# Gate products of the recurrent branch: four 64-wide blocks on the quadrants of the array in place of two 128-wide products

## The chip, the cores and the metric

The kernel runs on one core of one Trainium2 chip. The metric is the device time of one execution in microseconds. The kernel before has a median of 1052.98 us over 3 runs (1050.32 to 1054.1). TensorE is called PE in the profile, its weight loads PEld, VectorE DVE, ScalarE ACT, GpSimd POOL, and the queue of SyncE, which issues the transfers, SPq.

## The reference

One inference step of a one-layer hybrid decoder, for a prompt of 512 positions and 8 sampled sequences of 4 positions each (T = 544 columns in all). What matters here is the recurrent branch (an RG-LRU):

```python
xb = xf.reshape(B, T, RNN_BLOCKS, RNN_BLOCK_W)          # 16 blocks of 64
r = sigmoid(einsum('btnc,ncd->btnd', xb, w_a) + b_a)    # gate r: 64x64 product in each block
i = sigmoid(einsum('btnc,ncd->btnd', xb, w_x) + b_x)    # gate i: the same with other weights
log_a = LRU_C * r * log_sigmoid(lam)
a = exp(log_a)
u = sqrt(-expm1(2.0 * log_a)) * (i * xf)
h[t] = a[t] * h[t-1] + u[t]                             # scan over the positions
branch_a = (h * gelu(gr)) @ w_rnn_out
```

Around it stand one combined input projection, a sparse attention branch with an index, a merge, a feed-forward network (D_FF = 2816) and an embedding gate. Everything is float32.

## The kernel before, in words

**Tiles and units.** All large projections go through one stream of weight units. A unit is up to 8 chunks of 128x128 weights, loaded by SPq into a ring of 4 (`wraw`), rounded by ACT (`round_weights`, L613) to `whi`, and its rest computed by POOL (`lower_weights`, L1549) as `wlo`. ACT and POOL do this four units ahead of TensorE. TensorE (`run`, L1759) makes three products for each chunk (`whi` with the high and low part of the operand, `wlo` with the high part), each in two halves of 272 columns, into one of two pairs of PSUM banks (`psD`). A tile's pair of banks is free again when ACT or DVE has read it (`tile_read`). `run_around(n, work)` runs the first half of a unit, then `work`, then the second half.

**The recurrent branch.** D_RNN is 1024, so 8 chunks (c = 0 to 7) of 128 channels, each with two blocks of 64. Chunk c needs an `xr` tile (input of the branch) and a `gr` tile (its GeLU gate). TensorE's order for one chunk is: first half of the tile `xr` c+1, gate products `gate_sums(c, 0)`, second half of that tile, `gate_sums(c, 1)`, tile `gr` c. For c = 7, the first half of the tile `gr` 7 stands before its first gate product. Two other small jobs lie between: the turns `spt` and `spn` of the sampled attention after chunk 0's gates, and `new_values` with `past_values` before chunk 1 and again after chunk 2 (L1960, L1969).

**Gate products.** The weights `bd` hold, for each chunk and gate, a 128x128 matrix with two 64x64 blocks on its diagonal and zeros elsewhere. The operand `xc` has EO = 568 columns, taken as two halves of EH = 284 (k = 0, 1). Each half is a job of its own in the order `plan_aux`: its results go to one of two PSUM banks in turn (`psX[0]`, `psX[1]`, named by `bank(job)`). `start_job` waits until the job two before it was read, `end_job` tells the reader. Each float32 product shows in the trace as two records.

**ScalarE's order for a chunk.** `gates(c, 0)`: two Tanh instructions from PSUM into `rq` (L800, 128x284 each, scale and bias by partition), then the decay factor (Exp, L807) and a Tanh (L809); `final_states(c-1)` (L832 to L836); `gates(c, 1)`: two more of L800 into `ig`; the square root (L622); `y_upper` (L843); `conv_line(c+1)` (L773 to L781), which copies the `xr` tile out of PSUM and makes the first tap of the convolution; one rounding of weights (L613); `initial_states` (L826); the GeLU (L817); one more rounding. Three loads of function tables lie in each chunk.

**VectorE's order for a chunk.** `recurrence(c)`: L1281, L1286, L1287, then a wait for the square root, L1289, L1292, L1295, the convolution taps of chunk c+1 (L1152, three instructions), L1299, the scan L1305; `branch(c)`: L1313, L1314. After chunk 6 also `sample_own` (L1266). At the end stands `sample_out_lo` (L1271); TensorE's second attention product (L2023, in tile `ga` 0) needs the bank that it reads.

Of the kernel before, what the change touches and what calls it, by code (L numbers as in the profile page):

```python
# [11 lines left out]
ACT = mybir.ActivationFunctionType  # L12

P = 128
D = 1024
DC = D // P
# [8 lines left out]
HD = 64  # L25
# [25 lines left out]
EO = EXT - (CW - 1)  # L51
EH = EO // 2
# [115 lines left out]
def hybrid_decoder_step(nc, a, o):  # L168
# [13 lines left out]
    def place(name, shape, dt=F32, over=None, plus=0):  # L182

        size = 4 * int(np.prod(shape[1:]))
        if over is None:
            spot[name] = free[0]
            free[0] += (size + 31) // 32 * 32
        else:
            spot[name] = spot[over] + plus
        assert spot[name] + size <= 229344, (name, spot[name] + size - 229344)  # L190
        return nc.alloc_sbuf_tensor_at(name, shape, dt, offset=spot[name])
# [24 lines left out]
    lru = place("lru", [P, 8, DC])  # L216
    stat = place("stat", [P, 64])
    sstat = place("sstat", [P, 8])
    top8 = place("top8", [P, 8])
    pt = place("pt", [1, NB * NPG], I32)  # L220
    hmul = [place(f"hmul{i}", [P, T]) for i in range(2)]
# [37 lines left out]
    bd = place("bd", [P, DC, 2, P], F32, "iqT")  # L259
# [37 lines left out]
    with ctx:  # L297
# [62 lines left out]
        def bank(job):  # L360
            return psX[AUX[job] % 2]
# [23 lines left out]
        def got_job(eng, job):  # L385
            eng.wait_ge(aux_done, AUX[job] + 1)

        def read_job(ins, job):
            return ins.then_inc(aux_read[AUX[job] % 2], 1)
# [205 lines left out]
        def _(act):  # L595
            sc = nc.scalar
# [149 lines left out]
            def sample_exp(g):  # L746
                job_read(act, ("smask", g))
                sc.activation(ps_s[:, g, :], ps_s[:, g, :], ACT.Exp, bias=sstat[:, g:g + 1], scale=-1.0,
                              accum_out=sstat[:, 2 + g:3 + g]).then_inc(sexp_ok, 1)
# [34 lines left out]
            def gates(c, which):  # L784

                s = c % 2
                if which:
                    pass
                elif c >= 2:
                    act.wait_ge(hs_ok, c - 1)  # L790
                elif c == 0:
                    act.wait_ge(lru_v, 1)
                    job_read(act, ("vout", TT))
                else:
                    act.wait_ge(sp_ok, 2)
                for g, dst in (((0, rq[s]), (1, ig[s]))[which],):
                    for k in range(2):
                        job = ("gate", c, g, k)
                        got_job(act, job)
                        read_job(sc.activation(dst[:, EH * k:EH * (k + 1)], bank(job)[:, 0:EH], ACT.Tanh, scale=0.5,  # L800
                                               bias=lru[:, 4 + g, c:c + 1]), job)
                    if g == 0:
                        job_read(act, ("gate", c, 0, 0))
                        job_read(act, ("gate", c, 0, 1))
                        if c:
                            act.wait_ge(u_w, c)
                        sc.activation(dec[c // 5][:], rq[s][:], ACT.Exp, scale=lru[:, 6, c:c + 1],  # L807
                                      bias=lru[:, 6, c:c + 1]).then_inc(dec_ok, 1)
                        sc.activation(rq[s][:], rq[s][:], ACT.Tanh, scale=lru[:, 3, c:c + 1],  # L809
                                      bias=lru[:, 3, c:c + 1]).then_inc(q_lru, 1)  # L810
# [43 lines left out]

            sample_exp(0)
            sample_exp(1)
            for c in range(DC):
                gates(c, 0)
                if c >= 1:
                    final_states(c - 1)  # L860
                gates(c, 1)
                if c == 0:
                    sample_turned()
                lru_root(c)
                if c >= 1:
                    y_upper(c - 1)
                if c + 1 < DC:
                    conv_line(c + 1, NTH[("xr", c + 1, False)])
                    round_weights(n + RING)
                    n += 1  # L870
                initial_states(c)
                gelu_path(c, NTH[("gr", c, False)])
                round_weights(n + RING)
                n += 1
# [823 lines left out]
        def _(pe):  # L1698
            te = nc.tensor

            def start_job(job):

                n = AUX[job]
                if n >= 2:
                    pe.wait_ge(aux_read[n % 2], n // 2)
                return bank(job)

            def end_job(ins):
                return ins.then_inc(aux_done, 1)
# [236 lines left out]

            def gate_sums(c, g):

                for k in range(2):
                    b = start_job(("gate", c, g, k))  # L1950
                    if g == 0 and k == 0:
                        pe.wait_ge(xc_ok, c + 1)
                        if c == 0:
                            pe.wait_ge(bd_in, 64)
                    end_job(te.matmul(b[:, 0:EH], bd[:, c, g, :], xc[c % 2][:, EH * k:EH * (k + 1)],  # L1955
                                      start=True, stop=True))

            def new_values(g):

# [231 lines left out]
```

## Time and profile before

| | |
|---|---|
| median of 3 runs | 1052.98 us (1050.32 to 1054.1) |
| the profiled execution | 1053.02 us, of which the span of the core's instructions is 1051.3 us |
| mean granted clock of TensorE | 0.985 |
| stretch of the recurrent chunks | about 203 to 322.5 us of the span |
| gate products | 32 matmuls (64 records at L1955), 16 calls of `gate_sums` |

In the rows below, times are in us from the start of the span. A row of the timeline gives start, duration, engine, line, operation, output and inputs, shapes and the number of instructions that were merged into the row; in brackets stands how long the engine was idle before it and what ended that. In matmul rows, "128\*64" is the part of the array in use, rows by columns.

### The profile page before, as it was taken

The page shows a single profiled execution, that of the slowest core. Times are in us where ns is not written, and L with a number is a line of the kernel's source. Part 1 is how long each engine was busy: PE and PEld are TensorE (multiplying, and loading weights), DVE is VectorE, ACT ScalarE, POOL GpSimd, SP SyncE. Part 2 cuts the span into 40 slices and gives each one's busy share as a digit, 9 for nine tenths or more (in the row PEclk, how much of TensorE's full clock was granted, in tenths as well). Part 3 has the DMA queues.
Part 4 walks back from the last instruction along what each step waited for, and adds up shares of the span by engine and source line. Part 5 has one row for each costly group of instructions (what it writes and reads, how often), then busy time and mean ns, then how long its engine had stood idle before and what let it go on. Part 6 is the DMA issues. An engine that isn't in the chain of part 4 may idle for free.

```text
span 1051.3 us, 19192 instructions
## 1 busy us (share of the span) xinstructions
PE 1004.3 (96%) x7811; PEld 960.9 (91%) x7811; DVE 489.8 (47%) x762; ACT 421.0 (40%) x705; POOL 448.3 (43%) x301
## 2 busy tenths in 40 slices
PE   4889999899997999999999999999999999999997
PEld 3876898689996999899999999999999999999996
DVE  2315899478995344324454433343001333334464
ACT  5424333578994434333332522222112223233534
POOL 2513352156886445424541543433334433344530
PEclk9898999999998999999999999999999999999999
DMA  6633356542232431333252422322333232122502
GB/s 187 185 50 87 100 152 184 172 121 80 72 83 54 101 94 30 80 92 92 80 176 71 140 81 80 99 66 75 91 104 101 88 93 72 51 88 59 161 1 86
DMA packets 168751, 101.98 MB, mean 97 GB/s; under 512 B 12626, under 2 KB 160754, under 8 KB 168418
## 3 DMA queue, kind: packets, MB, share of 16 engines
q1 hardware_dynamic: 168674, 100.91, 34.2%
q8 instruction: 54, 0.88, 0.4%
q14 instruction: 23, 0.19, 0.1%
HBM read 93.26 MB, written 7.63 MB: 96 GB/s over the span
## 4 chain that ended last, share of the span: by engine, by line
PE 89%; ACT 3%; DVE 3%; DMA 3%; issue 1%; SPq 1%; POOL 1%; ACTq 0%; DVEq 0%
PE psD L1759 80%; PE psX L1713 2%; DMA wraw<-in_w_in 1%; PE held L1713 1%; PE psX L2023 1%; PE held L2047 1%; PE psX L1842 1%; PE psX L1955 1%; DMA prm<-in_state_rglru_h 1%; ACT whi L613 1%; DMA kpg<-in_cache_k 0%; PE held L1912 0%; PE held L1969 0%; POOL h_lo L1555 0%; DVE xc L1152 0%
## 5 line engine op out<-in xcount | busy, mean ns | idle before, releaser
L1549 POOL TENSOR_TENSOR wlo<-wraw,whi 128x1024 fp32r<-128x1024 f32 (+5 forms) x213 | 388.6, 1836 | 548.4 <-ACT whi L613 548.3
L1759 PE MATMUL psD<-h_hi,whi 128*128 128x272 f32 (+1 forms) x1616 | 344.9, 295 | 5.0 <-POOL h_lo L1555 3.1
L1759 PE MATMUL psD<-h_hi,wlo 128*128 128x272 f32 (+1 forms) x1616 | 336.4, 290 | 0.0
L1759 PE MATMUL psD<-h_lo,whi 128*128 128x272 f32 (+1 forms) x1616 | 335.8, 289 | 0.0
L1759 PEld LDWEIGHTS psD<-h_hi,whi 128*128 128x128 f32 (+1 forms) x1616 | 256.4, 190 | 17.4 <-issue 10.9
L1759 PEld LDWEIGHTS psD<-h_lo,whi 128*128 128x128 f32 (+1 forms) x1616 | 256.1, 190 | 0.0
L613 ACT CAST whi<-wraw 128x1024 fp32r<-128x1024 f32 (+4 forms) x165 | 154.8, 939 | 251.4 <-PE psD L1759 224.0
L1759 PEld LDWEIGHTS psD<-h_hi,wlo 128*128 128x128 f32 (+1 forms) x1616 | 254.5, 190 | 0.0
L1759 PE MATMUL psD<-act_hi,whi 128*128 128x272 f32 x672 | 140.8, 291 | 0.0
L1759 PE MATMUL psD<-act_hi,wlo 128*128 128x272 f32 x672 | 139.0, 288 | 0.0
L1759 PE MATMUL psD<-act_lo,whi 128*128 128x272 f32 x672 | 138.6, 288 | 0.0
L1759 PEld LDWEIGHTS psD<-act_hi,whi 128*128 128x128 f32 x672 | 105.6, 189 | 0.5 <-DVE act_lo L1384 0.3
L1759 PEld LDWEIGHTS psD<-act_lo,whi 128*128 128x128 f32 x672 | 105.6, 188 | 0.0
L1759 PEld LDWEIGHTS psD<-act_hi,wlo 128*128 128x128 f32 x672 | 105.0, 189 | 0.0
L1001 ACT ACTIVATE sg<-sg 128x544 f32<-128x544 f32 x22 | 14.5, 659 | 111.2 <-DVE sg L1450 111.2
L1499 DVE TENSOR_TENSOR x<-x,psD 128x544 f32<-128x544 f32 x16 | 11.5, 721 | 99.5 <-PE psD L1759 99.5
L1478 DVE TENSOR_TENSOR hmul<-sg,psD 128x544 f32<-128x544 f32 x22 | 15.9, 721 | 85.1 <-PE psD L1759 85.1
L1481 DVE TENSOR_TENSOR act_lo<-hmul,act_hi 128x544 f32 (+1 forms) x20 | 44.6, 2228 | 18.4 <-ACT act_hi L935 18.4
L1450 DVE TENSOR_TENSOR sg<-rb,psD 128x544 f32<-128x544 f32 x30 | 21.6, 721 | 67.4 <-PE psD L1759 67.4
L1335 DVE CUSTOM_DVE_ANT_0 pr<-psX,tm 128x128 f32<-128x128 f32 (+3 forms) x32 | 15.6, 489 | 63.7 <-PE held L1713 28.1
L892 ACT COPY pT<-held 128x128 f32<-128x128 f32 (+3 forms) x32 | 13.6, 424 | 46.4 <-PE held L1713 46.4
L916 ACT ACTIVATE sg<-psD 128x544 f32<-128x544 f32 x16 | 10.0, 625 | 50.0 <-PE psD L1759 50.0
(272 smaller groups left out, 975.2 us busy)
## 6 DMA issues: line engine op xcount, KB each, us to landing
wraw<-in_w_in SPq DMA_DIRECT2D x48, 512.0 KB, 4.6
wraw<-in_w_ffn_gate SPq DMA_DIRECT2D x22, 512.0 KB, 3.8
wraw<-in_w_ffn_up SPq DMA_DIRECT2D x22, 512.0 KB, 3.8
wraw<-in_w_ffn_down SPq DMA_DIRECT2D x16, 384.0 KB, 3.3
wraw<-in_w_ffn_down SPq DMA_DIRECT2D x16, 320.0 KB, 3.1
kpg<-in_cache_k SPq DMA_DIRECT2D x16, 256.0 KB, 3.0
wraw<-in_w_rnn_out SPq DMA_DIRECT2D x8, 512.0 KB, 5.0
wraw<-in_w_o SPq DMA_DIRECT2D x8, 512.0 KB, 5.9
```

The costliest lines, as they stand in the source:

```text
L613: sc.copy(whi[:, n % RING, 0:rc, 0:cc], wraw[:, n % RING, 0:rc, 0:cc]).then_inc(w_hi, 1)
L892: sc.copy(pT[s % 2][:, 0:block_of(s) + 1, :].rearrange("p k t -> p (k t)"), psX[2][:, 0:w])\
L1001: sc.activation(sg[k % 2][:], sg[k % 2][:], ACT.Silu).then_inc(act_ok, 1)
L1335: read_job(v.tensor_tensor_reduce(pr[st % 3][:, 0:w], bank(("qk", st))[:, 0:w], tm[st % 2][:, 0:w], -1.0, 3.0e38, ALU.add, ALU.min, stat[: ...
L1450: read_tile(v.tensor_tensor(two(sg[k % 2][:]), two(rb[:]), acc(t), ALU.mult), t)
L1478: read_tile(v.tensor_tensor(two(hmul[k % 2][:]), two(sg[k % 2][:]), acc(t), ALU.mult), t)
L1481: v.tensor_tensor(chunk(act_lo, f - 1), hmul[(k - 1) % 2][:], chunk(act_hi, f - 1).bitcast(F32), ALU.subtract).then_inc(f_lo, 1)
L1499: read_tile(v.tensor_tensor(two(x[:, j, :]), two(x[:, j, :]), acc(t), ALU.add), t)
L1549: ins = g_.tensor_tensor(wlo[:, s, r0:r1, 0:cc], wraw[:, s, r0:r1, 0:cc], whi[:, s, r0:r1, 0:cc].bitcast(F32), ALU.subtract)
L1713: return te.transpose(out, src, ident[0:rows, 0:rows])
L1759: ins = te.matmul(psD[0:cc, b0 + half, 0:HT], w[:, s, c, 0:cc], m[:, k0 + c, HT * half:HT * (half + 1)], start=(part == 0 and c == 0 and w ...
L1842: end_job(te.matmul(b[:, 0:P * (i + 1)], iqT[head_rows(h), h // 2, P * i:P * (i + 1)], ik2[head_rows(h), 0:P * (i + 1)], start=True, stop= ...
```

## The change

Each gate product of 128x128 (half of which are zeros) by 284 columns becomes two products of 64x64 blocks by the same 284 columns. For the first half of the columns (k = 0) block 0 stands on the upper left quadrant of the array and block 1 on the lower right, so that the results lie in PSUM as before. For the second half (k = 1) block 0 stands on the upper right quadrant and block 1 on the lower left: the results of block 0 come out on partitions 64 to 127 and those of block 1 on 0 to 63. The k = 1 results are read by two Tanh instructions of 64 partitions each, which take them crosswise, from partitions 64 to 127 into 0 to 63 of the destination and the other way round; the k = 0 results are read by one instruction as before. As the bias of such an instruction lies with its input, ScalarE makes a copy `crossed` of the two bias columns with the halves exchanged, in two small copies ahead of chunk 0. `gate_sums` now waits for both banks before its first product, not for each bank before its own.

```diff
+    crossed = place("crossed", [P, 2, DC])
...
                 for g, dst in (((0, rq[s]), (1, ig[s]))[which],):
-                    for k in range(2):
-                        job = ("gate", c, g, k)
-                        got_job(act, job)
-                        read_job(sc.activation(dst[:, EH * k:EH * (k + 1)], bank(job)[:, 0:EH], ACT.Tanh, scale=0.5,
-                                               bias=lru[:, 4 + g, c:c + 1]), job)
+                    job = ("gate", c, g, 0)
+                    got_job(act, job)
+                    read_job(sc.activation(dst[:, 0:EH], bank(job)[:, 0:EH], ACT.Tanh, scale=0.5,
+                                           bias=lru[:, 4 + g, c:c + 1]), job)
+                    job = ("gate", c, g, 1)
+                    got_job(act, job)
+                    for i, j in ((0, HD), (HD, 0)):
+                        ins = sc.activation(dst[i:i + HD, EH:EO], bank(job)[j:j + HD, 0:EH], ACT.Tanh, scale=0.5,
+                                            bias=crossed[j:j + HD, g, c:c + 1])
+                    read_job(ins, job)
...
             sample_exp(0)
             sample_exp(1)
+            act.wait_ge(lru_v, 1)
+            sc.copy(crossed[HD:P, :, :], lru[0:HD, 4:6, :])
+            link(sc.copy(crossed[0:HD, :, :], lru[HD:P, 4:6, :]))
...
             def gate_sums(c, g):
 
+                b = [start_job(("gate", c, g, k)) for k in range(2)]
+                if g == 0:
+                    pe.wait_ge(xc_ok, c + 1)
+                    if c == 0:
+                        pe.wait_ge(bd_in, 64)
                 for k in range(2):
-                    b = start_job(("gate", c, g, k))
-                    if g == 0 and k == 0:
-                        pe.wait_ge(xc_ok, c + 1)
-                        if c == 0:
-                            pe.wait_ge(bd_in, 64)
-                    end_job(te.matmul(b[:, 0:EH], bd[:, c, g, :], xc[c % 2][:, EH * k:EH * (k + 1)],
-                                      start=True, stop=True))
+                    for h in range(2):
+                        i, j = HD * h, HD * (h ^ k)
+                        ins = te.matmul(b[k][j:j + HD, 0:EH], bd[i:i + HD, c, g, i:i + HD],
+                                        xc[c % 2][i:i + HD, EH * k:EH * (k + 1)], start=True, stop=True,
+                                        tile_position=(i, j))
+                    end_job(ins)
```

## Rows read from the trace of the kernel before

**Rows 1.** The page: busy time of the engines, and the chain that ended last.

```profile
PE 1004.3 (96%) x7811; PEld 960.9 (91%) x7811; DVE 489.8 (47%) x762; ACT 421.0 (40%) x705; POOL 448.3 (43%) x301
PE psD L1759 80%; PE psX L1713 2%; DMA wraw<-in_w_in 1%; PE held L1713 1%; PE psX L2023 1%; PE held L2047 1%; PE psX L1842 1%; PE psX L1955 1%; DMA prm<-in_state_rglru_h 1%; ACT whi L613 1%; DMA kpg<-in_cache_k 0%; PE held L1912 0%; PE held
```

**Rows 2.** Windows: length; busy PE, PEld, DVE, ACT, POOL; PEclk; DMA share, GB/s.

```profile
278.40:292.40 14.00, 14.00 (x107) 13.60 (x106) 13.39 (x17) 12.98 (x24) 11.33 (x10) 1.00 0.28 76
306.40:322.50 16.10, 10.44 (x75) 9.35 (x73) 15.33 (x22) 11.38 (x24) 15.19 (x15) 0.91 0.38 98
```

**Rows 3.** Timeline of TensorE behind its last gate product.

```profile
322.53 0.79 PE L2023 MATMUL psX<-kT,qT 64*128 64x128 f32 x2 [5.31 <-DVE act_lo L1271]
```

**Rows 4.** Timeline of ScalarE, chunk 6 and the start of chunk 7.

```profile
293.06 0.92 ACT L800 ACTIVATE rq<-psX,lru 128x284 f32<-128x284 f32 x2 [0.74 <-PE psX L1955]
297.26 0.87 ACT L800 ACTIVATE ig<-psX,lru 128x284 f32<-128x284 f32 x2
299.44 0.68 ACT L622 ACTIVATE sq<-rq 128x568 f32<-128x568 f32 x1
307.01 0.92 ACT L800 ACTIVATE rq<-psX,lru 128x284 f32<-128x284 f32 x2 [0.72 <-PE psX L1955]
```

**Rows 5.** Timeline of VectorE, chunks 5 and 6.

```profile
295.00 1.68 DVE L1313 TENSOR_TENSOR hmul<-hs,hmul 128x512 f32<-128x512 f32 x1
300.23 0.78 DVE L1289 TENSOR_SCALAR rq<-dec 128x568 f32<-128x568 f32 x1
308.96 0.69 DVE L1313 TENSOR_TENSOR hmul<-hs,hmul 128x512 f32<-128x512 f32 x1
```

**Rows 6.** Timeline of TensorE around a call of the gate products.

```profile
220.28 0.42 PE L1759 MATMUL psD<-h_hi,wlo 128*128 128x272 f32 x2
220.53 1.12 PE L1955 MATMUL psX<-xc,bd 128*128 128x284 f32 x4
221.74 0.41 PE L1759 MATMUL psD<-h_lo,whi 128*128 128x272 f32 x2
```

**Rows 7.** Timeline of TensorE: column tiles of 32, and their last weight loads.

```profile
215.58 0.62 PE L1969 MATMUL held<-kpg,pts 128*32 128x512 f32 x2
215.59 0.62 PE L1969 MATMUL held<-vpg,pts 128*32 128x512 f32 x2
216.03 0.60 PE L1969 MATMUL held<-kpg,pts 128*32 128x512 f32 x2
...
215.62 0.12 PEld L1969 LDWEIGHTS held<-vpg,pts 128*32 128x32 f32 x2
```

**Rows 8.** Timeline of TensorE: row tiles of 64 (L1842), column tiles of 64 (L2047).

```profile
109.14 0.41 PE L1759 MATMUL psD<-h_hi,wlo 128*128 128x272 f32 x2
109.48 1.13 PE L1842 MATMUL psX<-ik,iqT 64*128 64x512 f32 x4
110.89 0.42 PE L1759 MATMUL psD<-h_lo,whi 128*128 128x272 f32 x2
...
460.40 1.09 PE L2047 MATMUL held<-pT,vtok 128*64 128x128 f32 x16 [1.70 <-ACT pT L892]
461.78 0.41 PE L1759 MATMUL psD<-act_lo,whi 128*128 128x272 f32 x2
```

**Rows 9.** ScalarE: one reading of 284 columns; 64 partitions read crosswise.

```profile
L800 ACT ACTIVATE ig<-psX,lru x16: 475/482/492, 206.3 to 311.6; 128x284 f32<-128x284 f32 x16
...
L681 ACT COPY ik<-psD 64x544 f32<-64x544 f32 x1 | 0.6, 605 | 0.0
```

**Rows 10.** Timeline of ScalarE: chunk 0, and the heads of chunks 1 and 3.

```profile
203.81 0.89 ACT L800 ACTIVATE rq<-psX,lru 128x284 f32<-128x284 f32 x2 [5.07 <-PE psX L1955]
206.31 0.86 ACT L800 ACTIVATE ig<-psX,lru 128x284 f32<-128x284 f32 x2
221.27 0.92 ACT L800 ACTIVATE rq<-psX,lru 128x284 f32<-128x284 f32 x2 [5.30 <-PE psX L1955]
251.22 0.92 ACT L800 ACTIVATE rq<-psX,lru 128x284 f32<-128x284 f32 x2 [1.99 <-PE psX L1955]
```

## The prediction

> **What bounds the kernel now.** I read the page first: TensorE is busy 96% of the span, the chain that ended last is 80% its large products, and the gate products are 1% of it [rows 1]. A saving on TensorE counts only where nothing else paces it. So next I cut the stretch of the recurrent chunks into windows. In chunk 5's 14.0 us TensorE is busy throughout, but VectorE is busy 13.39 us and ScalarE 12.98 us of the same stretch [rows 2]. Three engines run in step here, which the page's averages (47% and 40%) hide. Last the chain in order of time and the timeline of its end: from chunk 6's gate products the chain leaves TensorE and runs through ScalarE and VectorE to L1271, and TensorE, which had by then been idle for 5.31 us, goes on at 322.53 [rows 3]. What the branch costs is decided there, and by VectorE.
>
> How tight the three are: ScalarE waits 0.74 and 0.72 us for TensorE at the heads of chunks 6 and 7, which are 307.01 - 293.06 = 13.95 us apart [rows 4]; its own work in a loop is therefore 13.95 - 0.72 = 13.23 us. Its square root of chunk 6 ends at 299.44 + 0.68 = 300.12 [rows 4], and VectorE's L1289, which needs it, starts at 300.23 [rows 5]. From there to L1271 the timeline shows VectorE without a wait for anyone. What comes late to it in chunk 6 stays late.
>
> **TensorE's part.** Pairs of large products start 0.25 us apart. Without the gate call the second pair after the one at 220.28 would have started at 220.78; it starts at 221.74, so a call costs 0.96 us: four passes of 0.24 us and no change-over [rows 6]. After the change a call has 8 passes of 284 columns (4 products, two records each). Do they run side by side? Column tiles do: at L1969 the passes of four tiles start within 0.01 us of each other and the next ones 0.45 us later [rows 7], so 284 of those 512 columns take about 0.24 us, as above. Row tiles do as well: a call at L1842 has four passes of 512 columns, 4 x 0.43 = 1.72 us in turn, yet it moves the pairs behind it by only 110.89 - 109.64 = 1.25 us [rows 8]. The array split both ways is not in this trace. I take that it composes: 2 x 0.24 = 0.48 us of streaming.
>
> The change-over has a price. Of the 1.25 us at L1842, 0.86 is streaming; 0.39 is left [rows 8]. At L2047 16 passes of 128 columns stream two by two in 8 x 0.107 = 0.86 us; the second pair behind them starts 1.38 us after the first pass, where 0.86 + 0.25 would do, so the way out costs 0.27, and with the 0.09 us gap at L1842's way in (109.48 where 109.39 would do) it is 0.36 [rows 8]. A call then costs 0.48 + 0.36 to 0.39 = 0.84 to 0.87 us and saves about 0.1 us, not the half that the streaming suggests. I take 0.11, since two rows of the same kind agree. The bounds: no change-over at all gives 0.48 and saves 0.48; one unhidden load (0.12 us [rows 7]) on top of 0.87 gives 0.99 and loses 0.03.
>
> **ScalarE's part.** One reading of 284 columns lasts 0.482 us [rows 9] and two in a row 0.87 [rows 4], so one more in a row costs 0.39. Half the partitions do not look cheaper: a copy of 64x544, taken crosswise, lasted 0.605 us, while 284 columns on 128 partitions last 0.482 [rows 9], so the time goes by columns and a fixed part. I take the full 0.39; half of it would be the lower bound. Each gate call thus adds 0.39 us, 0.78 us a chunk. A bit comes back: the first pair of a chunk takes 0.92 us, since its second product comes late; arriving together they would take 0.87 [rows 4]. ScalarE's loop becomes 13.23 + 0.78 - 0.05 = 13.96 us, TensorE's 13.95 - 0.22 = 13.73. ScalarE takes over the pace, at about the old period. The two copies of `crossed` stand in 5.07 us for which ScalarE waits ahead of chunk 0 [rows 10] and cost nothing; without that cover they would be two short instructions, under 1 us (two readings), once.
>
> The rows above make the emptying of PSUM dearer by 0.39 us a call. The Trainium skill, TensorEngine Tiling (Array Packing), PSUM Bottleneck, speaks against the change in the same sense: tiling speeds up TensorE but not the emptying of PSUM, which may become the bottleneck. By that page alone the streaming would shrink and the pace would pass to ScalarE, which is what these rows give.
>
> **Chunk 0.** Here TensorE waits for ScalarE. The `ig` readings start at 206.31 behind three instructions [rows 10]; with three `rq` readings they start at 206.70. The turn `spt` needs the bank of the first of them (+ 0.39), `spn` that of the second: free at 206.31 + 0.39 + 0.48 = 207.18 now, at 206.70 + 0.78 + 0.48 = 207.96 then. TensorE leaves chunk 0 about 0.75 us late, and the saving of this chunk's two calls is lost in the waits.
>
> **Then chunk by chunk**, shifts against before. Chunk 1: ScalarE had 5.30 us of slack [rows 10], so TensorE decides: 0.75 - 0.11 = + 0.64. Chunk 2 (slack taken as the usual 0.73): ScalarE is ready at 0.64 - 0.73 + 0.73 = + 0.64, TensorE at 0.75 - 3 x 0.11 = + 0.42, so + 0.64. Chunk 3: ScalarE's slack was 1.99 [rows 10], so TensorE decides: 0.75 - 5 x 0.11 = + 0.20. Chunks 4 to 7 at ScalarE's pace, + 0.01 each: + 0.23 at chunk 6, + 0.24 at chunk 7. In chunk 6 both longer groups of readings stand ahead of the square root, which comes 0.23 + 0.78 = 1.0 us later; L1289 follows it, and the end of the branch comes 1.0 us later. Chunk 7's root, at 0.24 + 0.78, asks for the same.
>
> TensorE's own saving (13 calls from chunk 1 on, 1.4 us) only lengthens its idle stretch from 5.3 to about 5.3 + 1.4 - 0.75 + 1.0 = 7 us [rows 3]. The granted clock in this stretch is 0.91 of full already [rows 2], so the slow restart is in the time before too and I add nothing for it. Other waits that move, at no cost: GpSimd and the loads of weights stand behind ScalarE's roundings, about 1 us later but made four units of 6 us ahead; an `xr` tile's banks are read about 1 us later, and if TensorE stalls for them it eats only of its lead.
>
> **The sum.** The profiled execution took 1053.02 us, as good as the median: 1053.0 + 1.0 = 1054.0 us. Its own uncertainty: VectorE's instructions stretch when they fall on other work (L1313 took 1.68 us in chunk 5, 0.69 in chunk 6 [rows 5]), and a shift of 1 us deals these anew, by up to 2 us either way over the last two chunks. The three runs before spread over 3.8 us. About 0.5% (5.3 us) is what a measurement of this kernel can tell from no change.
>
> **Rivals.**
> 1. *Change-over nearly free*: 0.48 us a call. For it, only the bound; against it, both kinds of tiles pay 0.36 to 0.39 [rows 8]. TensorE is then at 0.75 - 0.48 = + 0.27 in chunk 1; ScalarE decides chunk 3 at 0.27 + 2 x 0.73 - 0.73 - 1.99 = - 0.99, chunk 6 at - 0.96, its root at - 0.96 + 0.78 = - 0.2: 1052.8 us. ScalarE gives all of it back. With readings at half the price or lucky overlaps on VectorE (- 2), down to 1050.8. Together 0.13.
> 2. *The halves take turns*, and it ends slower. The tiles of k = 0 and k = 1 share rows of the array; if each pair ran only after the other, a call would be 4 x 0.24 + 0.37 = 1.33 us, or 1.45 with an unhidden load: + 0.37 to + 0.49. It decides from about 1.1 us a call on, where TensorE's loop passes ScalarE's new one. Chunk 7 then starts at 0.75 + 13 x 0.37 to 0.49 = + 5.6 to + 7.1, its root 0.78 later: 1059.4 to 1060.9. Against it: the four tiles at L1969 share all rows and start together [rows 7]. Chance 0.10. The Trainium skill, TensorE: Matmul & The Clock Gate, What overlaps and what doesn't, says that weight loads overlap running products only when the row group differs; by that rule this rival comes true. The trace disagrees for column tiles: the last load of four tiles on the same rows starts at 215.62, within 0.04 us of their first pass [rows 7].
> 3. *No overlap on quadrants*: 8 x 0.24 + 0.37 = 2.29 us, + 1.33 a call, in all 0.75 + 13 x 1.33 + 0.78 = + 18.8: 1072 us. Only the lack of a row with the array split both ways speaks for it. 0.05.
>
> **How the numbers follow.** My forecast 0.66 (1052 to 1056.5), rival 1 0.13, rival 2 0.10, rival 3 0.05, something not named 0.06, half to each side. Faster by over 0.5% means below 1047.7 and has only the unnamed: 0.03. Slower by over 0.5% (above 1058.2) is rivals 2 and 3 and 0.02 of the unnamed: 0.17. Within: 0.80. The range 1050.5 to 1059.7 holds rival 1 and the near edge of rival 2 and leaves out some 0.17.
>
> **What would show it.** Right: a gate call moves the pairs of L1759 behind it by 0.8 to 0.9 us; the passes at L1955 start in two groups of four; three readings take about 1.26 us; ScalarE's idle time ahead of `rq` is gone in chunks 4 to 7; VectorE waits for the root in chunk 6; TensorE is idle for 6.5 to 7.5 us ahead of L2023, which goes on near 323.5. Wrong: passes in four groups or one by one, a ScalarE that still waits, L2023 before 321, or a longer stretch at a low clock after it.

## The result, and the profile of the changed kernel

The changed kernel takes 1061.01 us (median of 4 runs, 1059.94 to 1062.07), the kernel before, measured beside it, 1052.08 us (4 runs, 1050.32 to 1054.1): ratio 1.0078, 95% interval 1.0064 to 1.0092. It is slower by some 0.8%, clear of the noise, and the time lies above the predicted range. The profiled execution took 1060.13 us; its span is 1058.4 us where it was 1051.3.

The page of the changed kernel, busy time of the engines, against [rows 1]:

```profile
PE 1004.8 (95%) x7875; PEld 956.2 (90%) x7875; DVE 489.0 (46%) x762; ACT 431.3 (41%) x723; POOL 448.1 (42%) x301
```

ScalarE has 10.3 us more work in 18 more instructions, and TensorE's busy time has not fallen. The line hardly shows a loss of 7 us; the stages do.

TensorE of the changed kernel, timeline around a call of the gate products (as [rows 6]), then chunk 0, then a call late in the branch and the restart (as [rows 3]):

```profile
221.89 0.41 PE L1768 MATMUL psD<-h_hi,wlo 128*128 128x272 f32 x2
222.23 0.71 PE L1966 MATMUL psX<-xc,bd 64*64 64x284 f32 x8
...
223.23 0.42 PE L1768 MATMUL psD<-h_lo,whi 128*128 128x272 f32 x2
...
202.44 0.71 PE L1966 MATMUL psX<-xc,bd 64*64 64x284 f32 x8
204.93 0.71 PE L1966 MATMUL psX<-xc,bd 64*64 64x284 f32 x8 [1.78 <-ACT rq L805]
206.93 1.63 PE L1722 MATMUL psX<-ident,ps_s 128*128 128x128 f32 x6 [1.29 <-ACT ig L800]
208.22 0.80 PE L1768 MATMUL psD<-h_hi,whi 128*128 128x272 f32 x2
208.81 0.66 PE L1768 MATMUL psD<-h_lo,whi 128*128 128x272 f32 x2
209.27 0.66 PE L1768 MATMUL psD<-h_hi,wlo 128*128 128x272 f32 x2
...
295.92 0.71 PE L1966 MATMUL psX<-xc,bd 64*64 64x284 f32 x8 [0.68 <-DVE xc L1161]
...
327.78 0.79 PE L2036 MATMUL psX<-kT,qT 64*128 64x128 f32 x2 [4.25 <-DVE act_lo L1280]
```

Chunk 0 of the kernel before, for the waits and the distances:

```profile
203.04 1.12 PE L1955 MATMUL psX<-xc,bd 128*128 128x284 f32 x4
204.35 1.22 PE L1955 MATMUL psX<-xc,bd 128*128 128x284 f32 x4 [0.19 <-ACT rq L800]
206.84 0.87 PE L1713 MATMUL psX<-ident,ps_s 128*128 128x128 f32 x6 [1.26 <-ACT ig L800]
207.47 0.50 PE L1759 MATMUL psD<-h_hi,whi 128*128 128x272 f32 x2
```

Three things are to be seen. A call moves the second pair behind it to 223.23, where 221.89 + 0.50 would do without it: it costs 0.84 us, as forecast. In chunk 0 the longest wait is 1.78 us, where it was 1.26, and pairs of large products start 0.46 us apart in place of 0.25: TensorE came back from its waits at a lower clock. And late in the branch TensorE now waits 0.68 us for `xc`, the convolution's result on VectorE, and restarts at 327.78, where it had been 322.53.

ScalarE of the changed kernel, timeline of chunk 5 and the head of chunk 6, against [rows 4]:

```profile
282.27 0.50 ACT L800 ACTIVATE rq<-psX,lru 128x284 f32<-128x284 f32 x1
282.79 1.00 ACT L805 ACTIVATE rq<-psX,crossed 64x284 f32<-64x284 f32 x2
...
287.07 0.49 ACT L800 ACTIVATE ig<-psX,lru 128x284 f32<-128x284 f32 x1
287.58 1.00 ACT L805 ACTIVATE ig<-psX,crossed 64x284 f32<-64x284 f32 x2
...
296.72 0.50 ACT L800 ACTIVATE rq<-psX,lru 128x284 f32<-128x284 f32 x1
```

No row has a bracket: ScalarE waits for nobody, from head to head 14.45 us (before 13.95). The readings of a gate last 282.79 + 1.00 - 282.27 = 1.52 us; two lasted 0.87 to 0.92, and the forecast for three was 1.26. Each starts 0.50 to 0.52 us after the one ahead, which is its whole duration: the overlap that made "one more in a row" cost 0.39 is gone.

VectorE of the changed kernel, chunk 5, against [rows 5]:

```profile
290.68 0.46 DVE L1298 TENSOR_SCALAR rq<-dec 128x568 f32<-128x568 f32 x1 [0.65 <-ACT sq L623]
...
292.92 2.85 DVE L1161 SCALAR_TENSOR_TENSOR xc<-xe,prmT,xc 128x568 f32<-128x568 f32 x3 [0.34 <-ACT xc L782]
```

VectorE waits for the square root and for the first tap, both of ScalarE. TensorE waits for VectorE, ahead of the first gate call of chunks 2 and 4 to 7. Only at the heads of chunks 1 and 3 does ScalarE still wait for TensorE, 6.10 and 1.10 us. Everywhere else the branch runs at ScalarE's pace.

Windows of the changed kernel: chunk 0, the end of the branch (as the second of [rows 2]), the output turns at the end of the program:

```profile
202.40:210.40 8.00, 4.93 (x33) 3.54 (x33) 1.95 (x3) 6.76 (x12) 0.00 (x0) 0.79 0.57 165
...
311.20:327.70 16.50, 10.73 (x74) 9.74 (x74) 15.21 (x22) 12.51 (x26) 14.38 (x15) 0.85 0.35 97
...
1046.95:1058.40 11.45, 6.90 (x34) 6.25 (x34) 4.15 (x8) 4.33 (x7) 0.00 (x0) 0.65 0.51 196
```

The same windows of the kernel before, chunk 0 and output turns:

```profile
203.00:211.00 8.00, 6.55 (x44) 5.42 (x43) 2.43 (x6) 6.71 (x14) 0.00 (x0) 1.00 0.56 170
1041.10:1051.30 10.20, 5.52 (x34) 4.56 (x34) 3.87 (x8) 4.32 (x7) 0.00 (x0) 0.77 0.57 218
```

The granted clock was 1.00 in chunk 0 and is 0.79. In the output turns (the last transposes on TensorE, ahead of the outputs), which the diff doesn't touch, the same 34 matmuls take 6.90 us in place of 5.52, at 0.65 in place of 0.77 of the 2.4 GHz.

**Where the time came from.** Cutting both timelines at the first reading of chunks 0, 1 and 7, at the restart, at the next product of L2036 and at the sums ahead of the output turns gives the table. All kernels of the study stand in it (one profiled execution each, us):

| kernel | chunk 0 | chunks 1 to 7 | 7 to restart | restart to next | middle | output turns |
|---|---|---|---|---|---|---|
| before | 17.46 | 85.74 | 15.52 | 8.35 | 710.22 | 10.20 |
| changed | 19.76 | 88.16 | 16.59 | 8.94 | 710.23 | 11.45 |
| before, again | 17.47 | 85.74 | 15.51 | 8.49 | 710.25 | 10.25 |
| changed, again | 20.93 | 88.15 | 16.60 | 9.60 | 710.22 | 11.27 |
| e1 TensorE's part | 18.91 | 84.41 | 15.63 | 9.46 | 710.24 | 11.39 |
| e9 ScalarE's part | 19.78 | 88.72 | 16.59 | 8.86 | 710.24 | 11.46 |
| e2 straight halves | 19.69 | 88.53 | 16.29 | 9.07 | 710.23 | 11.46 |
| e15 upper half first | 18.63 | 88.43 | 16.58 | 8.82 | 710.22 | 11.47 |
| e3 halves by columns | 17.67 | 86.25 | 15.65 | 8.25 | 710.20 | 10.23 |
| e10 third full reading | 19.67 | 86.03 | 16.25 | 9.10 | 710.24 | 11.48 |
| e12 the same, with quadrants | 19.58 | 86.55 | 15.97 | 8.15 | 710.26 | 11.41 |
| e4 chunk 0 as before | 17.62 | 87.89 | 16.59 | 8.60 | 710.23 | 10.17 |
| e8 bank by bank | 19.76 | 88.13 | 16.58 | 8.98 | 710.22 | 11.47 |
| e5 before, readings behind its end | 17.46 | 85.74 | 15.52 | 8.60 | 710.23 | (see text) |

From before to changed: chunk 0 + 2.30, the loops + 2.42, the tail + 1.07, behind the restart + 0.59, output turns + 1.25; with 0.54 less ahead of chunk 0, whose start lies anywhere from 201.6 to 204.9 us in these profiles, that is + 7.1 us. The middle, 710 us, is the same to 0.06 us in all rows. e5's last column has no value, since its added readings stand behind the turns; TensorE's own part of the turns, from the sums to the end of the last turn, takes 5.27 us in it, 5.51 in the kernel before and 6.90 in the changed one.

### The profile page after: what moved, and what is told of

Its sections match the earlier page's. It is cut to its first block, busy times and chain, and to the rows that moved or that the text cites. A ratio compares the mean times of both kernels' runs of the same rounds, so it can differ in the third digit from the quotient of the medians.

```text
span 1058.4 us, 19348 instructions
## 1 busy us (share of the span) xinstructions
PE 1004.8 (95%) x7875; PEld 956.2 (90%) x7875; DVE 489.0 (46%) x762; ACT 431.3 (41%) x723; POOL 448.1 (42%) x301
## 4 chain that ended last, share of the span: by engine, by line
PE 67%; DVE 1%; ACT 1%; issue 0%; DVEq 0%; ACTq 0%
PE psD L1768 63%; PE psX L2036 1%; PE held L1722 1%; PE held L2060 1%; PE psX L1722 0%; DVE act_lo L1393 0%; ACT whi L614 0%; PE psX L2109 0%; PE psD L1722 0%; PE held L2118 0%; DVE hs L1314 0%; ACT L623 0%; ACT L813 0%; DVE hmul L1322 0%; ACT ig L805 0%
```

## The experiments

**e1: TensorE's part alone.** The products stand on the quadrants, the readings are the two full ones of before (the k = 1 halves stay exchanged).

```diff
-                    for i, j in ((0, HD), (HD, 0)):
-                        ins = sc.activation(dst[i:i + HD, EH:EO], bank(job)[j:j + HD, 0:EH], ACT.Tanh, scale=0.5,
-                                            bias=crossed[j:j + HD, g, c:c + 1])
-                    read_job(ins, job)
+                    for k in range(2):
+                        job = ("gate", c, g, k)
+                        got_job(act, job)
+                        read_job(sc.activation(dst[:, EH * k:EH * (k + 1)], bank(job)[:, 0:EH], ACT.Tanh, scale=0.5,
+                                               bias=lru[:, 4 + g, c:c + 1]), job)
```

> TensorE's part alone: the four quadrant products of the change, read by ScalarE as before in one instruction of 128 partitions for each half, so that the k = 1 values of two blocks stand exchanged. Theory A (the loss is ScalarE's: a half-partition reading is paced at 0.51 us and lengthens the loop of chunks from 13.95 to 14.46 us): heads of the chunks 13.7 to 13.95 us apart, TensorE's gate call 0.84 us, time within 2 us of the kernel before (1050 to 1054). Theory B (the loss is TensorE's: waits for both banks, change-over, clock): most of the 9 us stays, 1057 or more.

1053.37 us (10 runs, 1052.08 to 1057.88), ratio 1.0011, interval 0.9996 to 1.0027: no difference. Timeline of ScalarE, heads of two chunks:

```profile
277.19 0.89 ACT L801 ACTIVATE rq<-psX,lru 128x284 f32<-128x284 f32 x2 [0.59 <-PE psX L1961]
...
290.98 0.89 ACT L801 ACTIVATE rq<-psX,lru 128x284 f32<-128x284 f32 x2 [0.61 <-PE psX L1961]
```

TensorE still sets the pace here, and its saving counts: heads 13.79 us apart, the loops 1.33 us shorter. But chunk 0 is 1.45 us longer, the stretch behind the restart 1.1 us and the output turns 1.2 us. Timeline of TensorE in chunk 0:

```profile
202.59 0.71 PE L1961 MATMUL psX<-xc,bd 64*64 64x284 f32 x8 [1.15 <-ACT rq L801]
```

The shorter calls leave TensorE idle for 1.15 us between ScalarE's readings, where it was 0.19, and in this execution its clock is down (0.50 from 204 to 206 us). What was saved in one stage was lost in others.

**e9: ScalarE's part alone.** Products of before, three readings, two of them crosswise with the bias from `crossed`. This exchanges the k = 1 halves.

```diff
-                        ins = te.matmul(b[k][j:j + HD, 0:EH], bd[i:i + HD, c, g, i:i + HD],
-                                        xc[c % 2][i:i + HD, EH * k:EH * (k + 1)], start=True, stop=True,
-                                        tile_position=(i, j))
+                    end_job(te.matmul(b[:, 0:EH], bd[:, c, g, :], xc[c % 2][:, EH * k:EH * (k + 1)],
+                                      start=True, stop=True))
```

> ScalarE's part alone: the 128x128 products of the kernel before, each waiting for its own bank, and the change's three readings of a gate, two of them crosswise (the k = 1 values stand exchanged). Theory A: heads of the chunks 14.4 to 14.5 us apart, time 1057 to 1061. Theory B: heads 13.95 to 14.1 us apart, time 1052 to 1055.

1059.45 us (4 runs), ratio 1.0067, interval 1.005 to 1.0084. Timeline of ScalarE:

```profile
283.89 0.50 ACT L800 ACTIVATE rq<-psX,lru 128x284 f32<-128x284 f32 x1
...
298.37 0.50 ACT L800 ACTIVATE rq<-psX,lru 128x284 f32<-128x284 f32 x1
```

Most of the loss (0.67% of 0.78%), at the same pace (14.48 us) and without one quadrant. The readings make it.

**e2: straight halves.** As e9, but partitions 0 to 63 and then 64 to 127 are read without crossing.

```diff
+                    for i in (0, HD):
+                        ins = sc.activation(dst[i:i + HD, EH:EO], bank(job)[i:i + HD, 0:EH], ACT.Tanh, scale=0.5,
+                                            bias=lru[i:i + HD, 4 + g, c:c + 1])
```

> The kernel before with the k = 1 half of each gate read by two instructions of 64 partitions, straight, not crosswise (the same values). If reading a half of the partitions is what costs 0.51 us (split theory): the same as with crosswise readings, 1057 to 1061, and three readings in 1.52 us. If the crossing costs it: each 0.39 us, three readings in 1.26 us, loop near 14.0 us, 1053 to 1055.

1059.73 us (4 runs), ratio 1.0068, interval 1.0051 to 1.0085: the crossing as such is not the cause. Timeline of ScalarE:

```profile
269.04 0.50 ACT L799 ACTIVATE rq<-psX,lru 128x284 f32<-128x284 f32 x1
269.45 1.00 ACT L804 ACTIVATE rq<-psX,lru 64x284 f32<-64x284 f32 x2
...
273.63 0.20 ACT L841 COPY stO<-hs 128x8 f32<-128x8 f32 x1
273.86 0.50 ACT L799 ACTIVATE ig<-psX,lru 128x284 f32<-128x284 f32 x1
```

The lower half starts 0.41 us after the full reading, so it overlaps it; the upper half doesn't overlap the lower. Three readings take 1.41 us, where 1.52 was expected, and yet the heads are 14.51 us apart. The difference is in two gaps elsewhere, ahead of L799's `ig` (273.63 to 273.86, 0.23 us, where it is 0.11 in the changed kernel) and ahead of the first copy out of PSUM (L775, again 0.23 us).

**e5: readings by themselves.** Behind the end of the kernel before, series of four Tanh readings of 284 columns from PSUM, each followed by a short one.

```diff
+            for r in range(4):
+                sc.activation(many[HD:P, 4 + r, 0:EH], src[HD:P, 0:EH], ACT.Tanh, scale=0.5, bias=bias[HD:P])
...
+            for r in range(4):
+                i = HD * (r % 2)
+                sc.activation(more[i:i + HD, r, 0:EH], src[i:i + HD, 0:EH], ACT.Tanh, scale=0.5, bias=bias[i:i + HD])
```

> The kernel before with, behind its last output, series of four readings of 284 columns from PSUM on ScalarE: 128 partitions; 0 to 63; 64 to 127; crosswise; halves in turn straight; halves in turn crosswise; 96 partitions; 0 to 63 and 128 without a bias by partition. Split theory: the start-to-start distance is 0.39 us only for 128 partitions and 0.50 to 0.52 us for all 64-partition series, straight or crosswise. Crossing theory: 0.39 straight, 0.51 crosswise. Change-of-range theory: 0.39 for four in a row on the same partitions, 0.51 only where the range changes from one to the next.

One run, 1068.39 us with the added readings. Timeline of ScalarE, in order: all partitions; the lower half four times; the upper half four times; lower half crosswise to the upper four times, and the short reading behind it; lower and upper in turn, straight; in turn, crosswise.

```profile
1049.29 1.66 ACT L1065 ACTIVATE many<-psX,lru 128x284 f32<-128x284 f32 x4
...
1051.14 1.64 ACT L1068 ACTIVATE many<-psX,lru 64x284 f32<-64x284 f32 x4
...
1052.96 1.65 ACT L1071 ACTIVATE many<-psX,lru 64x284 f32<-64x284 f32 x4
...
1054.92 1.64 ACT L1074 ACTIVATE many<-psX,lru 64x284 f32<-64x284 f32 x4
1056.57 0.27 ACT L1075 ACTIVATE spare<-psX,lru 128x8 f32<-128x8 f32 x1
1056.87 2.00 ACT L1078 ACTIVATE more<-psX,lru 64x284 f32<-64x284 f32 x4
...
1059.18 2.00 ACT L1082 ACTIVATE more<-psX,lru 64x284 f32<-64x284 f32 x4
```

This settles the price. Four readings take 1.64 to 1.66 us, 0.385 from start to start with the last lasting 0.50, whatever their number of partitions, and crossing costs nothing, as long as all have the same first partitions. When the first partition changes from one to the next they take 2.00 us, 0.50 each, straight or crosswise. Half the partitions save nothing, nor do 96 of 128 (four take 1.65 us).

Input and output change together in the two series in turn. Behind the fourth series only the output changes, from partition 64 to 0, and the short reading starts at 1056.57, when the reading ahead of it has ended (1054.92 + 1.64); behind the second series, where nothing changes, it starts 0.11 us before that end (1052.67 against 1051.14 + 1.64). So a change of the output alone costs the overlap too. Two last series had no bias by partition: four readings take 1.28 us on 64 partitions and 1.30 on 128.

**e15: upper half first.** e2 with the two halves in the other order.

```diff
-                    for i in (0, HD):
+                    for i in (HD, 0):
```

> The kernel with the k = 1 bank read in two straight halves, but partitions 64 to 127 before 0 to 63. Readings with the lower half first left two gaps of 0.23 us where others are 0.11: ahead of the first ig reading (L799, behind L841) and ahead of the first copy out of PSUM (L775, behind L773). Theory, a memory: an instruction loses its overlap of 0.11 us when its input in PSUM starts on another partition than the last input that ScalarE read from PSUM, even with instructions between them that read SBUF; both gaps are where partition 0 follows upper halves that were read last. With the upper half first, the last reading starts on partition 0: three readings take 1.52 us in place of 1.41, both gaps are 0.11, and the heads are 1.52 + 0.11 - 2 x 0.12 later or earlier, in all some 0.02 us a chunk from the kernel with the lower half first (14.47 to 14.51 us apart), as the changed kernel has them (14.46). Rival, only the instruction directly ahead counts: the readings take 1.52 us all the same, the two gaps stay at 0.23, and the heads come out 14.7 us apart.

One run, 1058.91 us, as its theory said. Timeline of ScalarE:

```profile
266.65 0.50 ACT L799 ACTIVATE rq<-psX,lru 128x284 f32<-128x284 f32 x1
267.18 1.00 ACT L804 ACTIVATE rq<-psX,lru 64x284 f32<-64x284 f32 x2
...
271.35 0.20 ACT L841 COPY stO<-hs 128x8 f32<-128x8 f32 x1
271.46 0.49 ACT L799 ACTIVATE ig<-psX,lru 128x284 f32<-128x284 f32 x1
```

The readings take 1.53 us, the gap ahead of `ig` is back to 0.11, and heads are 14.47 to 14.50 us apart. So the instruction directly ahead is not what counts: L799 is compared with the last reading from PSUM, with seven instructions between the two. The gap ahead of L775 is back to 0.11 us as well; it is a copy without a bias, so the place of the bias is not what counts. A bank of which only the upper half was read last makes the next reading from PSUM lose its overlap.

The Trainium skill, VectorE: DVE Perf Modes, Two Vector instructions with no wait between them, states such a rule for VectorE: an instruction starts only when all earlier ones have finished if its input starts in another group of 32 partitions than the last input from the same memory, or its output in another than the last output there. e2, e5 and e15 show ScalarE doing the same, with partitions 0 and 64, at 0.11 us a time.

**e3: halves by columns.** Products of before; the second half of the columns is read in two instructions of 142 columns on all partitions.

```diff
+                    for i in (0, EH // 2):
+                        ins = sc.activation(dst[:, EH + i:EH + i + EH // 2], bank(job)[:, i:i + EH // 2], ACT.Tanh,
+                                            scale=0.5, bias=lru[:, 4 + g, c:c + 1])
```

> The kernel before with the k = 1 half of each gate read by two instructions of 142 columns on all 128 partitions. Theory A: three readings last 0.39 + 2 x 0.27 = 0.93 us start to start and some, so ScalarE's loop is 13.23 + 2 x 0.15 to 0.27 = 13.5 to 13.8 us, below TensorE's 13.95: heads stay 13.95 apart, and only the root of the last chunks comes 0.3 to 0.5 us later; time within 1 us of the kernel before, 1052 to 1053.5. Rival (an instruction more is what costs, not its length): heads 14.4 or more, 1058 or more.

1053.45 us (10 runs), ratio 1.0006, interval 0.9996 to 1.0016. Timeline of ScalarE:

```profile
265.91 0.50 ACT L799 ACTIVATE rq<-psX,lru 128x284 f32<-128x284 f32 x1 [0.44 <-PE psX L1960]
266.33 0.65 ACT L804 ACTIVATE rq<-psX,lru 128x142 f32<-128x142 f32 x2
```

A third instruction, but the same columns and the same first partition: 1.07 us, and ScalarE still waits for TensorE. The number of instructions alone costs next to nothing in the time. The last three loops take 14.12 us, though, where 13.95 was expected; why was not looked into.

**e10 and e12: the forecast's own price.** A third reading of all 128 partitions into memory that nobody uses, 0.39 us from start to start: e10 with the products of before, e12 with those of the change (k = 1 halves exchanged). As the memory is shared, both also have a wait of ScalarE ahead of chunk 0 that the diff below does not show (`act.wait_ge(slogit_q, 2)`, before `sample_exp`).

```diff
+                        if k:
+                            sc.activation(spare[g][:], bank(job)[:, 0:EH], ACT.Tanh, scale=0.5, bias=lru[:, 4 + g, c:c + 1])
```

> The kernel before with a third reading of 128 partitions in each gate call (the k = 1 bank is read once more, into memory that nothing uses): the forecast's own price, an additional 0.39 us a call, without change of partitions and without TensorE's part. Theory A (the price decides: ScalarE's loop 13.23 + 0.78 = 14.0 us against 13.95): heads of the chunks 14.0 us apart, time 1.0 to 2.5 us over the kernel before, 1053.5 to 1055. Rival (any third reading brings the whole loss, whatever it lasts): heads 14.4 or more, 1058 or more.

> The forecast's own sum as a kernel: TensorE's part of the change (quadrants, both banks waited for) with three readings a call that keep to 128 partitions (k = 0, the k = 1 bank into memory that nothing uses, the k = 1 bank), 0.39 us more a call; the k = 1 values stand exchanged. Theory A: the stretch from chunk 1's first reading to chunk 7's takes 86.0 us, as with the third reading alone (TensorE's saving is worth nothing once ScalarE paces), chunk 0 takes 19.5 us with the fall of the clock, the end of the branch is 3 to 3.5 us later than before, time 1055 to 1057. Rival (TensorE's saving counts): the stretch takes 84.4 to 85.2 us, time 1053 to 1054.5.

e10: 1055.92 us (6 runs), ratio 1.0034, interval 1.002 to 1.0048. e12: 1056.98 us (9 runs, 1056.33 to 1058.89), ratio 1.0044, interval 1.0033 to 1.0056. Timeline of ScalarE in e12:

```profile
282.20 0.50 ACT L804 ACTIVATE rq<-psX,lru 128x284 f32<-128x284 f32 x1 [0.60 <-PE psX L1965]
```

TensorE's call ahead of it in e12:

```profile
281.40 0.71 PE L1965 MATMUL psX<-xc,bd 64*64 64x284 f32 x8 [0.79 <-DVE xc L1160]
```

At its own price for the readings the forecast of 1054.0 would still have been 3 us low. e10's loops (14.00 us) fit the forecast's 13.96, but chunk 0 costs 2.2 us in place of 0.75, and the time is 0.9 us above the 1055 expected. e12, with the cheaper calls, has loops 0.5 us longer than e10 in all: two of its six take 14.56 and 14.55 us. There TensorE waits 0.79 us for `xc` and ScalarE then 0.60 for TensorE, which the sum did not have. `xc` is late there, and two steps of VectorE ahead of it last longer than in the next loop: L1297 0.85 us against 0.46, the three taps 3.37 against 2.86. Why they stretch in two of the loops is open.

**e4: chunk 0 as before.** For c = 0 the old products and readings, for the rest the change.

```diff
+                if c == 0:
+                    for k in range(2):
+                        b = start_job(("gate", c, g, k))
...
+                        end_job(te.matmul(b[:, 0:EH], bd[:, c, g, :], xc[c % 2][:, EH * k:EH * (k + 1)],
+                                          start=True, stop=True))
+                    return
```

> The kernel after, with chunk 0's two gate calls (products and readings) as before and chunks 1 to 7 as changed. Theory A (chunk 0 costs on its own: from the first reading of chunk 0 to that of chunk 1 the kernel after takes 19.76 us and the one before 17.46, through waits for the longer readings and the fall of TensorE's clock that follows; the rest is ScalarE's loop): chunk 0 takes 17.3 to 17.6 us again, pairs of L1768 behind it 0.25 us apart, heads of the chunks still 14.46 apart, and the time is 2 us less than the kernel after, near 1059. Rival (the loop of ScalarE absorbs what chunk 0 gives back, or the loss lies elsewhere): no difference to the kernel after, 1061.

1057.2 us (4 runs, 1054.97 to 1059.3), ratio 1.0055, interval 1.0038 to 1.0071. So 2.4 us (by the two ratios) to 4 us (by the medians) of the loss come from what happens in chunk 0; 2 were expected. Timeline of TensorE:

```profile
202.65 1.22 PE L1972 MATMUL psX<-xc,bd 128*128 128x284 f32 x4 [0.19 <-ACT rq L802]
205.13 0.88 PE L1729 MATMUL psX<-ident,ps_s 128*128 128x128 f32 x6 [1.26 <-ACT ig L802]
...
206.10 0.41 PE L1775 MATMUL psD<-h_lo,whi 128*128 128x272 f32 x2
206.35 0.41 PE L1775 MATMUL psD<-h_hi,wlo 128*128 128x272 f32 x2
```

The waits are 0.19 and 1.26 us as before, pairs stay 0.25 us apart, and the output turns are back at 10.17 us. The execution shown is the fastest of the four (1054.97); whether the turns are as short in the other three is not known.

**e8: bank by bank.** The change, but each bank is waited for ahead of its own products.

```diff
-                b = [start_job(("gate", c, g, k)) for k in range(2)]
...
                 for k in range(2):
+                    b = start_job(("gate", c, g, k))
```

> The kernel after, with gate_sums waiting for each bank ahead of that bank's own two products, not for both ahead of all four. Theory A: the second bank of chunk 0 is still read only by the crosswise readings, so TensorE's idle time there and the fall of its clock stay nearly whole; chunk 0 takes 19.5 to 19.8 us and the time stays within 1 us of the kernel after, 1060 to 1061.5. Rival (it is the common wait that costs chunk 0 its 2.3 us): chunk 0 takes 17.5 to 18 us, time near 1059.

1059.87 us (4 runs), ratio 1.008, interval 1.0063 to 1.0097; chunk 0 takes the same 19.76 us. Timeline of TensorE:

```profile
202.71 0.70 PE L1966 MATMUL psX<-xc,bd 64*64 64x284 f32 x4 [0.67 <-ACT rq L800]
203.74 0.70 PE L1966 MATMUL psX<-xc,bd 64*64 64x284 f32 x4 [0.33 <-ACT rq L805]
```

The one wait of 1.78 us becomes two of 0.67 and 0.33 us, and chunk 0 is no shorter for it. The joint wait costs nothing.

**e13 and e14: both kernels again, one execution each.**

> The kernel before once more, for a second profile. The output turns at the very end took 10.2 us in three profiles (before, chunk 0 as before, column pieces) and 11.4 to 11.5 in six others. Theory A (chance of the moment at which TensorE's clock falls): either value can come. Rival (the turns' clock hangs on what chunk 0 did): 10.2 us again, and no fall of the clock behind chunk 0.

> The kernel after once more, for a second profile. Chunk 0 takes 19.8 us, the stretch of chunks 1 to 7 88.2 us, the tail of chunk 7 16.6 us, all within 0.2 us. The output turns take 10.2 or 11.5 us by theory A (chance), 11.5 by the rival.

1052.28 and 1063.4 us. The loops and the tail repeat to 0.01 us. Chunk 0 of the changed kernel doesn't: 20.93 in place of 19.76 us, with the clock at half from 208 to 214 us, in the first profile only from 207 to 210. The kernel before stays at 17.47 us and full clock. The output turns take 10.25 and 11.27 us, near the first profile of each kernel, which speaks against chance alone.

## Why the prediction was wrong, step by step

**TensorE's part: right.** 0.84 us a call against 0.84 to 0.87. The eight passes start in two groups of four, 0.26 to 0.29 us apart, so the four quadrants run side by side, and the change-over has its price. That two measured kinds of tiles compose was assumed; it came true. Rivals 2 and 3 are refuted, and so is rival 1's free change-over. The Trainium skill, TensorE: Matmul & The Clock Gate, What overlaps and what doesn't, says that a weight load overlaps running products only when its row group differs. It does not hold here: the tiles of k = 0 and k = 1 share rows, and their passes start within 0.02 us of each other. As rival 2 reads that rule, a call would cost 1.33 us.

**ScalarE's price: the step that failed.** "One more in a row costs 0.39" was taken from readings with the same first partition. With the change three readings take 1.52 us in place of 0.87 to 0.92, 0.62 us more a call. The mechanism (ScalarE takes over the pace) was right, the size was not: loop 13.23 + 2 x 0.62 = 14.47, measured 14.45 to 14.47 in four of the six, forecast 13.96. The trace of before already had the row, one line above the one that I quoted; timeline of ScalarE in the kernel before:

```profile
69.59 0.61 ACT L680 COPY ik<-psD 64x544 f32<-64x544 f32 x1
70.21 0.60 ACT L681 COPY ik<-psD 64x544 f32<-64x544 f32 x1
```

0.62 us from start to start at a duration of 0.61: no overlap. L681 writes the upper half from the same input as L680, so its output starts on another partition. I compared durations, where the pace is made by the distance of starts. The Trainium skill, TensorEngine Tiling (Array Packing), PSUM Bottleneck, had the right direction: the emptying of PSUM took over. Its reason, a faster TensorE, is not the one here: e9 has the same pace with TensorE's part as before.

**Shifts chunk by chunk.** Forecast + 0.64 at chunk 1, then shrinking to + 0.24 at chunk 7. Instead chunk 0 alone added 2.30, and the loops added 2.42 us: 0.51 to 0.52 in four of the six, 0.79 in one, and - 0.43 in the one with slack (chunk 2 to 3). The forecast had - 0.44 there; "TensorE decides" did hold at chunks 1 and 3, where ScalarE waits for it. But a dependence was missing: TensorE's next call waits for VectorE's taps, which wait for ScalarE. These waits (0.68 to 0.99 us, ahead of five of the seven chunks) hold TensorE to ScalarE's pace, and in the four loops from chunk 3 on its saving wins next to nothing (14.45 to 14.47 us in three of them, e9 without it 14.48 to 14.50).

**Chunk 0.** The wait was forecast at 0.75 us. From the first gate product to the next large product it was 4.43 us and is now 208.22 - 202.44 = 5.78, + 1.35. Most of it is the same wait at the true price of the readings: e15, with readings of that length and no fall of the clock, has + 1.17 both there and over chunk 0. The rest of the + 2.30 is the clock, which I had not looked at in this place: e9 has e15's waits in chunk 0 to 0.01 us (0.19, 0.28 and 1.34), its clock fell, and its chunk 0 is 1.15 us longer. The clock fell in eight of the nine profiles with three slow or extra readings or shorter calls in chunk 0, and in none of the five others; in e15, the ninth, it didn't. The waits alone do not tell when it falls.

**Root and end.** From chunk 7's head to its root it takes 1.24 us more than before (forecast 0.78), again 2 x 0.62. VectorE, which had not waited there before, now waits 0.63 us for this root, so that chunk 7's root and not chunk 6's sets the end. From the root's end to L1280 VectorE took 7.95 us, before 8.13; the forecast's "what comes late stays late" held. The restart came at 327.78, not near 323.5: 4.18 at chunk 7's head + 1.24 - 0.18 on VectorE = 5.24, measured 5.25.

**"I add nothing for the clock" failed twice.** The stretch behind the restart costs 0.59 us more and the output turns 1.25 us. The turns go with what chunk 0 did 840 us earlier: 10.2 us (and e5's 5.27) in the five profiles with chunk 0 at 17.5 to 17.7 us, 11.3 to 11.5 in the nine with a longer one, and e4 differs from the changed kernel in chunk 0 alone. How the two are tied is open. The fall of the clock in chunk 0 is not the link: e15 had no fall and 11.47 us.

**The size of each.** The wrong price of the readings explains 1061.0 - 1057.0 = 4.0 us (changed kernel against e12; 3.6 by the ratios). The other 3.0 are e12 against the forecast. By stages of the one profiled execution they are + 1.5 us in chunk 0 (2.12 against 0.64), + 1.2 in the loops (0.81 against - 0.40), + 1.2 in the output turns and - 0.5 in the two stages between. No kernel tried beats the one before. By the rule that e5 and e15 show, the crosswise readings need at least two changes of first partition a call, in any order of the three; no other order was run.

## What to carry to other kernels

Price an added instruction by the distance of starts in a row of instructions like it, with the same first partitions as it will have, not by durations or by any neighbour of the same shape. When an engine is made faster in a loop that three engines share, ask which of the others is within the saving of it, and follow the dependences once round the loop before a saving is counted. Where short calls alternate with readings of another engine, a saving lengthens the idle pieces, and a fall of the clock can take back the saving, as in e1.

## What the runs showed of the hardware

- ScalarE's consecutive readings of 284 columns overlap by 0.11 us (0.385 us from start to start, 0.50 alone) unless the first partition differs (0 against 64) from the last one, for the input in PSUM (e2, e15) or the output in SBUF (e5, L680 and L681); then 0.50. A reading of 64 or 96 partitions costs as much as one of 128, and a crosswise one as much as a straight one.
- 8 passes of 284 columns on the four quadrants (two groups of four) cost 0.84 us between large products. The groups start 0.26 to 0.29 us apart.
- TensorE's clock fell from full to half (1.2 GHz) in chunk 0 in eight profiles whose longest wait there was 1.29 to 1.78 us, and stayed full in six with 1.26 to 1.35 us. In one kernel it was down for 3 us in one execution and for over 6 in another.
